# A state-space layer's tail: another home for the last decay rows, the projection's steps one output tile at a time, squares added on GpSimd, weight loads moved

## The reference, cut to what matters

```
y_f, s_f = ssd_chunked(xs, dt[:, :, 0], a[0], bm, cm, init_f)
y_b, s_b = ssd_chunked(flip(xs), flip(dt[:, :, 1]), a[1], flip(bm), flip(cm), init_b)
y = y_f + flip(y_b, 1) + xs * d_skip[:, None]
y = y.reshape(b, n, 2048) * silu(z)
y = rmsnorm(y, norm_g)
return y @ w_out, s_f, s_b          # w_out: 2048 x 1024
```

## Time and profile before

| | us |
|---|---|
| median of 3 runs | 1938.73 (1938.47 to 1939.22) |
| profiled execution | 1939.55, span 1937.7 |
| PE busy | 1842.9 (95%) |
| DVE, ACT, POOL busy | 1010.2, 605.0, 1192.1 (52%, 31%, 62%) |
| mean granted clock of TensorE | 0.982 |
| PE's longest waits in all: on the weight split (L997) | 22.3 in 7 |
| PE waits at the start of the kernel (parameters, sums) | 9.9 and 9.1 |
| PE busy in 1200 to 1410 | 181.4 of 210; from 1350 on every 10 us are 10.00 busy |
| SP's issues: rows of chunk 0 of group 3; T_O+2, T_O+3; rows of chunk 1; reload of `xT` | 1224.10; from 1233.58; 1254.69; 1327.22 |

### The profile page before, as it was taken

One profiled execution on the slowest core, in us unless ns is written; L12 is line 12 of the kernel. 1 busy time (PEld: TensorE's weight loads), 2 busy tenths in 40 slices (PEclk: granted clock), 3 DMA queues, 4 the chain that ended last, 5 costly groups with the idle time before them and its releaser, 6 DMA issues. The chain is left out here.

```text
span 1937.7 us, 33472 instructions
## 1 busy us (share of the span) xinstructions
PE 1842.9 (95%) x12857; PEld 1737.2 (90%) x12857; DVE 1010.2 (52%) x1600; ACT 605.0 (31%) x1141; POOL 1192.1 (62%) x869
## 2 busy tenths in 40 slices
PE   5999999999999999989999999976999999999997
PEld 3878899999999999989898898956999999999996
DVE  4555654563256146373666766694345623651553
ACT  4344421220022012145556657382112201220221
POOL 2533366777777777736455455514877777777773
PEclk8999999999999999999999999997999999999998
DMA  9631164424243433524333333223222222222221
GB/s 329 204 124 48 32 210 153 162 69 159 66 162 93 135 108 109 172 82 130 98 111 108 98 109 99 90 74 120 66 76 65 76 75 68 75 76 75 67 62 69
DMA packets 256189, 208.68 MB, mean 108 GB/s; under 512 B 7352, under 2 KB 235741, under 8 KB 255453
## 3 DMA queue, kind: packets, MB, share of 16 engines
q1 hardware_dynamic: 255373, 204.69, 33.5%
q10 hardware_dynamic: 720, 2.62, 0.3%
HBM read 196.63 MB, written 10.67 MB: 107 GB/s over the span
## 5 line engine op out<-in xcount | busy, mean ns | idle before, releaser
L993 POOL TENSOR_SCALAR w_hi<-raw 128x512 fp32r<-128x512 f32 (+1 forms) x432 | 643.6, 1507 | 716.8 <-PE ps L1027 530.9
L997 POOL TENSOR_TENSOR w_lo<-raw,w_hi 128x512 fp32r<-128x512 f32 (+1 forms) x432 | 555.5, 1307 | 0.0
L1027 PE MATMUL ps<-h_hi,w_hi 128*128 128x322 f32 (+1 forms) x1432 | 343.8, 321 | 4.5 <-DVE h_lo L2358 2.9
L1027 PE MATMUL ps<-h_lo,w_hi 128*128 128x322 f32 (+1 forms) x1432 | 328.5, 311 | 0.0
L1027 PE MATMUL ps<-h_hi,w_lo 128*128 128x322 f32 (+1 forms) x1432 | 328.2, 310 | 0.0
L1027 PEld LDWEIGHTS ps<-h_hi,w_hi 128*128 128x128 f32 x1432 | 241.5, 190 | 20.6 <-issue 18.3
L1027 PEld LDWEIGHTS ps<-h_hi,w_lo 128*128 128x128 f32 x1432 | 242.0, 189 | 0.0
L1027 PEld LDWEIGHTS ps<-h_lo,w_hi 128*128 128x128 f32 x1432 | 240.8, 189 | 0.0
L2249 DVE SCALAR_TENSOR_TENSOR xT<-ps,mod,xT 128x128 f32 (+1 forms) x112 | 56.6, 547 | 269.1 <-PE ps L1027 263.5
L1027 PE MATMUL ps<-g_hi,w_hi 128*128 128x322 f32 (+1 forms) x816 | 189.5, 314 | 4.5 <-POOL w_lo L997 3.1
L1027 PE MATMUL ps<-g_lo,w_hi 128*128 128x322 f32 (+1 forms) x816 | 187.6, 311 | 0.0
(11 more groups left out here) (354 smaller groups left out, 3138.4 us busy)
## 6 DMA issues: line engine op xcount, KB each, us to landing
raw<-in_ffn_w_up SPq DMA_DIRECT2D x88, 512.0 KB, 3.9
ada<-in_ada_w SPq DMA_DIRECT2D x40, 1024.0 KB, 6.5
raw<-in_ssd_w_in SPq DMA_DIRECT2D x40, 512.0 KB, 4.0
raw<-in_ffn_w_down SPq DMA_DIRECT2D x32, 512.0 KB, 3.9
R<-scr_acs SPq DMA_DIRECT2D x22, 512.0 KB, 5.3
raw<-in_att_w_in SPq DMA_DIRECT2D x16, 512.0 KB, 7.9
ada_att<-in_ada_w SPq DMA_DIRECT2D x8, 1024.0 KB, 7.2
raw<-in_ssd_w_out SPq DMA_DIRECT2D x16, 512.0 KB, 3.9
```

Source lines behind the costliest of these rows:

```text
L993: nc.gpsimd.tensor_scalar(w_hi[j % 2][:, a_:b_, :], raw[j][:, a_:b_, :], 1.0, None, ALU.mult).then_inc(w_hi_done, 1)
L997: ins = nc.gpsimd.tensor_tensor(w_lo[j % 2][:, a_:b_, :], raw[j][:, a_:b_, :], w_hi[j % 2][:, a_:b_, :].bitcast(F32), ALU.subtract)
L1027: ins = mm(out[:, cols], w[slot][:, k, :], x[:, cols], start=first and k == 0 and i == 0, stop=last and k == n - 1 and i == 2)
```

## The change

The schedule of `seg` and `yout`:

```diff
-            put(*slots[at - (0 if (g, c) == (GROUPS - 1, 1) else 2)], "seg", g, c)
+            put(*slots[at - 2], "seg", g, c)
...
-            for k, i in enumerate((9, 10, 11, 11, 13, 14, 14, 16, 17, 17, 19, 20)):
-                put(*slots[i], "yout", g, k)
+            todo = iter([(m, k) for m in range(2) for k in range(8)] + [(0, k) for k in range(8, 12)])
+            for i, n in ((9, 2), (10, 2), (11, 3), (13, 2), (14, 4), (16, 2), (17, 2), (19, 1), (20, 2)):
+                for _ in range(n):
+                    put(*slots[i], "yout", g, *next(todo))
```

A `yout` event is now one k step of one output tile (6 matmuls instead of 12): first tile 0, k 0 to 7, then tile 1, k 0 to 7, then tile 0, k 8 to 11. By slots: 9 (0,0) (0,1); 10 (0,2) (0,3); 11 (0,4) (0,5) (0,6); 13 (0,7) (1,0); 14 (1,1) to (1,4); 16 (1,5) (1,6); 17 (1,7) (0,8); 19 (0,9); 20 (0,10) (0,11). Behind the list:

```diff
-            for k in range(12, 16):
-                y_part(k)
+            for m, k in ((1, 8), (1, 9), (1, 10), (1, 11), (0, 12), (0, 13), (0, 14), (0, 15), (1, 12), (1, 13), (1, 14),
+                         (1, 15)):
+                y_part(m, k)
```

The home of `R_last` and of the odd squares, and the wait of the first load:

```diff
-        y_sums, y_sq = bT[0], (cT[0], x_tok[0][:, :, :].rearrange("p c n -> p (c n)")[:, 0:W])
+        y_sums, y_sq = bT[0], (cT[0], at("y_sq1", [P, W], F32, h_at + 12 * W * 4)[0])
...
-        R_last = at("R_last", [P, 2, GH, P], F32, aligned(h_at + 12 * W * 4))[0]
+        R_last = x_tok[0][:, :, :].rearrange("p c n -> p (c n)")[:, 0:2 * GH * P].rearrange(
+            "p (a b c) -> p a b c", a=2, b=GH)
...
                 if n == N_MID + 1:
-                    sp.wait_ge(mm_done, T_E + 40)
+                    sp.wait_ge(*ssd_end(("yd", GROUPS - 2, CHUNKS - 1)))
+                    sp.wait_ge(st_done, CS_AT[("csf", GROUPS - 2, 3)] + 1)
...
-                        after = () if n == N_MID - 2 else (n + 1, n + 2) if n in (N_MID - 1, N_MID) else (n + 2,)
-                        for i in after if n != N_MID - 1 else (n + 1,):
+                        after = () if n == N_MID - 2 else (n + 1, n + 2) if n == N_MID - 1 else (n + 2,)
+                        for i in after:
```

The rows of chunk 1 of group 3 are thus issued right behind those of chunk 0, in `beside(36)`, between the loads of T_O+1 and T_O+2. The odd squares' buffer is now the place of `y_hi` tile 12, so ACT waits before it:

```diff
                 act.wait_ge(*ssd_end(("yd", k // 4, 4)))
+                if k == 12:
+                    act.wait_ge(y_added, 11)
...
                         A_(yg[:, m, :], acc(e % 2), ACT.Silu).then_inc(acc_free_act, 1)
+                        if e == 39:
+                            A_(small[:, 15:16], ident[:, 0:1], ACT.Exp)
```

SP's order of the weight loads and the reload:

```diff
-            sp.wait_ge(*ssd_end(("yd", 3, 4)))
-            sp.wait_ge(st_stored, 128)
-            sp.dma_start(xT[:, :, :], scr_x).then_inc(x_back, 16)
-            with sp.Fori(1, 4) as i:
+            for j in range(4):
+                if j == 2:
+                    sp.wait_ge(*ssd_end(("yd", 3, 4)))
+                    sp.wait_ge(st_stored, 128)
+                    sp.dma_start(xT[:, :, :], scr_x).then_inc(x_back, 16)
+                load(j, T_O + 4 + j, w_so[:, (j % 2) * 8:(j % 2) * 8 + 8, (2 + j // 2) * P:(3 + j // 2) * P])
+            with sp.Fori(2, 4) as i:
```

POOL adds the squares of k = 1 to 11, between the splits; DVE keeps 12 to 15:

```diff
-            splits(T_E, T_END - 8)
+            def add_y_square(k):
+
+                pool.wait_ge(y_sqd, k + 1)
+                if k > 1:
+                    pool.wait_ge(y_added, k - 1)
+                nc.gpsimd.tensor_tensor(y_sums[:, :], y_sums[:, :], y_squares(k), ALU.add).then_inc(y_added, 1)
+
+            splits(T_E, T_O)
+            for j in range(2):
+                split(j, T_O + j, T_O // 4, KD)
+            for k in range(1, 8):
+                add_y_square(k)
+            split(2, T_O + 2, T_O // 4, KD)
+            for k in range(8, 10):
+                add_y_square(k)
+            split(3, T_O + 3, T_O // 4, KD)
+            for k in range(10, 12):
+                add_y_square(k)
+            splits(T_O + 4, T_END - 8)
...
-                if k:
-                    if k > 1:
-                        dve.wait_ge(y_added, k - 1)
+                if k >= 12:
+                    dve.wait_ge(y_added, k - 1)
                     tt(y_sums[:, :], y_sums[:, :], y_squares(k), ALU.add).then_inc(y_added, 1)
```

More of the change, by code:

```diff
@@ L1363, in _, with y_part @@
             ada_turn(ADA_LAST).then_inc(ada_cols, 1)
-            def y_part(k):
+            def y_part(m, k):
                 pe.wait_ge(y_ready, k + 1)
                 part = k // KD
[L1370 to L1377, removed]
+                if k % KD == 0:
+                    pe.wait_ge(w_split, T_O + 2 * part + m + 1)
+                if k == 0:
+                    pe.wait_ge(*acc_free(A_O + m - 2))
+                ins = steps(m, m, y_of(part), (k % KD,), first=part == 0, last=part == 1)
+                if k % KD == KD - 1:
+                    ins.then_inc(mm_done, 1)
             def ssd_begin(key):
@@ L1438, in _ @@
                 if kind == "yout":
-                    y_part(ev[2])
+                    y_part(ev[2], ev[3])
                 elif kind == "trB":
```

## The result

The changed kernel takes 1942.03 us (median of 19 runs, 1939.17 to 1948.39), the kernel before, run beside it, 1939.22 (19 runs). The ratio is 1.0018 with a 95% interval of 1.0011 to 1.0026: slower by 0.18%, with 2.8 us between the medians. One of the 19 runs of the kernel before took 2272.55 us, far above all others, and the ratio, which is of the fast runs, leaves it out. The time lies in the predicted range, and the likeliest case, no change, did not come: the interval lies above 1. The profiled execution took 1941.05, its span is 1939.2 (before: 1939.55 and 1937.7).

The account below looks back on a forecast made before the run. PE, 95% busy, was taken to bound the kernel, DVE setting the pace between waits in the state-space layer's end; +13.5, -12.0 and -1.8 gave -0.2 us, 1938.5 on the median, 8-in-10 range 1932.0 to 1943.5.

Parts of the forecast that it names:

- E1: Eviction of chunk 1 of group 3; forecast at 1275.8, 0.5 us later than before.
- The add's price: Squares' adds on POOL beside DVE's two-input SBUF work: 1.3 us lost each, 3.6 us taken for three in chunk 1.
- the home's 1.1 us: New home of R_last alone gives 1.1 us of the 5.4 us wait before chunk 1's product; DVE is next late.
- E1 to E2: Evictions of chunk 1 to chunk 2: PE waits for y_lo 4, stage 21.45 us, chunk 2's eviction 7.0 later than before.
- E2 to E3: Evictions of chunk 2 to chunk 3: PE waits for y_lo 7, stage 20.9 us against 14.36, +6.5.
- E3 to S: Eviction of chunk 3 to start of output tile 2: 28.4 us against 40.35, gain 12.0, weight waits mostly covered.
- S: Start of output tile 2, 1344.94 before; forecast at about 1346.
- the last term of the sum: Behind the start of output tile 2: wait of two us instead of 7.76 spares the low clock, -1.8 us.
- Z: Trace marker, no forecast: the RECIPROCAL of the last sums of squares ahead of the outputs.
- (a): Rival: adds on POOL cost DVE nothing, meeting its pauses and PSUM reads; sum -6.3, 1932.4 us; chance 0.23.
- (b): Rival: reordered steps don't hold PE up, three weight waits (19.15) and their low clock go; about 1917; chance 0.07.
- (c): Rival: slower by TensorE's clock, low for 6.1 us behind long waits, also behind short ones; +5.6, 1944.3; chance 0.15.

Follow-up runs that it names:

- b_home: The kernel before with only the new home of R_last and odd squares, its earlier load and exp, and the dummy Exp; 1938.71 us, ratio 1.0000.
- a_mix: The kernel after with projection steps in pairs to k 7 and tile by tile from k 8, adds still on POOL; 1934.95 us, ratio 0.9971.
- mix_dve: a_adds_on_dve with projection steps in pairs to k 7 and tile by tile from k 8; 1928.20 us, ratio 0.9940.
- a_adds_on_dve: The kernel after with the sums of squares back on DVE for all k, none on POOL; 1937.49 us, ratio 0.9994.
- a_fill2: The kernel after with spare matmuls in its two waits for y_lo, 28 before step (0,4) and 32 before (0,7); 1936.67 us, ratio 0.9984.
- a_early: The kernel after with 30 spare matmuls ahead of PE's first instruction, none near the tail; 1938.19 us, ratio 0.9997.
- mix_dve_early: mix_dve with 9 spare matmuls ahead of PE's first instruction; 1925.07 us, ratio 0.9928.
- a_fill: The kernel after with 9 spare matmuls in PE's wait before output tile 2; 1939.03 us, ratio 1.0003.
- b_early: The kernel before with 30 spare matmuls ahead of PE's first instruction, none near the tail; 1935.78 us, ratio 0.9979.
- b_fill: The kernel before with 30 spare matmuls in PE's wait of 7.76 us before output tile 2; 1934.54 us, ratio 0.9974.
- a_fill_all: The kernel after with spare matmuls in all its waits of the tail; 1935.58 us, ratio 0.9979.
- b_fill_all: The kernel before with spare matmuls in all its long waits of the tail; 1932.92 us, ratio 0.9965.
- a_old_steps: The kernel after with the projection's steps again in pairs, k by k, for both output tiles; 1943.03 us, ratio 1.0018.

## Why the prediction was wrong, by its own steps

**E1 right.** Predicted +0.5, measured +0.19 from chunk 0's product. The add's price was right in kind and size: 3.6 us lost to three adds forecast, 3.4 measured. By the exclusive lock of the Trainium skill ("SBUF — State Buffer", "Who interferes with whom") it would have been 4.7, an estimate: three adds of 1.55. The trace agrees that the two engines hold each other up, but the measured 1.1 each stay below that. b_home shows the home's 1.1 us: E1 1.0 earlier (19.67 against 20.69), and a wait of 5.38 still before chunk 1, released by DVE.

**E1 to E2 and E2 to E3 right.** Forecast 21.45 and 20.9, measured 21.39 and 20.56; before 14.95 and 14.36. PE started at E1+13.0 (forecast 13.8) and E2+10.7 (10.55).

**E3 to S right in kind, 1.2 us too short.** Forecast 28.4, measured 29.6, so the gain there was 10.8 us and not 12.0: POOL's split of T_O+3 ended at E3+11.4 as forecast, ACT's `y_hi` 12 came at E3+15.7 (15.0), T_O+4's split began at E3+24.1 (23.0), and PE waited 2.08 us (2). S moved +2.07, forecast +1.6. The rows of after for the two (E3 at 1315.37):

```profile
1331.05 0.83 ACT L1820 ACTIVATE y_hi<-yg,par 128x642 fp32r<-128x642 f32 x1 [13.96 <-POOL bT L1023]
```

```profile
1339.50 2.96 POOL L1000 TENSOR_SCALAR w_hi<-raw 128x512 fp32r<-128x512 f32 x2 [8.54 <-PE ps L1052]
```

**The step that failed** is the last term of the sum: "Two us of wait instead of 7.76 also spare the low clock after S: 1.8." In the profiled run the low clock under the work behind S grew instead, from 2.9 to 6.8 us, and S to the end took 1.48 us longer: 3.3 of the 3.75 us between the sum on record (-0.2) and the +3.55 counted from chunk 0's product. Before's wait of 7.76 us had taken 3.9 us of the low stretch into itself; after's of 2.08 us took none. The argument was a single row, the wait of 1.62 us that had left the pace. After a wait of 2.08 us, three traces show the low clock behind S (after, a_mix, mix_dve) and four don't (a_adds_on_dve, a_fill2, a_early, mix_dve_early). A short wait neither spares the clock nor costs it for certain. The term could come out from about -1.5 to +3 (S to Z 574.7 or 579 against before's 576.1); -1.8 lay beyond the better end of that, and I booked it as certain. With the middle, about +0.75, the sum would have been +2.3.

One trace of each kernel can't carry this alone. a_early and a_fill have after's tail up to S, b_early and b_fill before's. S lies 93.64 and 94.23 us behind chunk 0's product in the first two, 89.16 and 90.39 in the others: 4.5 and 3.8 later, not 2.07. Part of that is the clock between E2 and E3, low for 5.8 and 6.2 us behind the wait for `y_lo` 7 (2.8 in after's trace); these stages took 21.87 and 22.08 us instead of 20.56. a_early's wait and the end of its low stretch:

```profile
1305.58 0.90 PE L1052 MATMUL ps<-y_hi,w_hi 128*128 128x322 f32 x2 [7.92 <-DVE y_lo L2452]
```

```profile
1311.00:1312.00 1.00, 1.00 (x8) 1.00 (x7) 0.00 (x0) 0.00 (x0) 1.00 (x2) 0.83 0.07 16
```

There S to Z is 1.5 us shorter than b_early's, nearly what the term had said, but the gain from E3 to S is 9.1 us. So from E3 to the end, where the sum had -13.8 (-12.0 and -1.8), the pair before and after shows -9.3 and the pair b_early and a_early about -11: too much gain was booked there in either, at S or behind it.

**The rivals.** (a) is refuted by a_adds_on_dve: POOL's adds cost 0.24%. (b) is refuted by the trace: the waits for `y_lo` came, 7.06 and 7.92 us. (c), slower by the clock, named the right sign and the right places (the low level came behind both short waits, 1325.4 to 1328.8 and 1345.9 to 1352.7), but isn't the whole cause. Its long restarts stayed low for 4.8 and 2.8 us, less than its 6.1; in a_early's and a_fill's traces the second reached 5.8 and 6.2. And pairs of kernels with the same fillers, or with fillers in all long waits, keep most of the difference: a_early against b_early 0.9997 to 0.9979 (2.4 us), a_fill_all against b_fill_all 0.9979 to 0.9965 (2.7 us); the intervals overlap in both pairs, and a_fill_all's trace still has two short low stretches, from 1289.6 and 1327.1, where b_fill_all's has none. What stays there is the place of the waits: S 4.3 us later in a_fill_all than in b_fill_all, since in before's order fillers win back 3 us of S and in after's 0.7. I had given the change credit for -12.0 at S against +13.6 at E3; that they nearly cancel was right (-10.8 against +12.8), and the 0.18% is what is left of it, with a clock term whose sign I had wrong. The runs, each with its mean granted clock, tell roughly how the two share it. Within after (19 runs) as within before (108 runs, taken beside the experiments) a run takes 1.2 us less for each 0.001 of clock that it has more; the mean clocks are 0.9803 and 0.9811, the mean times 3.3 us apart. By that, an estimate from clocks listed to 0.001, the clock holds about 1 us of the difference and the waits 2.3. No experiment shows the two apart.

**The range.** It held the median, by its width: the forecast, 1938.5, was 3.5 us below. The chance for slower, 0.18, was too small, since it rested on the one row of 1.62 us against the clock.

## What to carry to other kernels

Before steps are reordered, write beside each slot which operand it needs and when that is made; a step put ahead of its operand moves a wait, and where PE waits either way only the shorter sum of waits counts (mix_dve: pairs while operands come late, tile by tile once a buffer has to be freed: -0.6%, with 9 fillers -0.8%, 1922.70 us, the fastest here). Work given to GpSimd isn't free while VectorE reads two SBUF inputs: each add of 0.74 us saved cost 1.1. A shorter wait doesn't shorten the low clock in step, for a long wait takes part of the low stretch into itself; a term that rests on the clock's level behind a wait belongs into the range, not into the sum, and an experiment that adds instructions needs a twin that adds them elsewhere.

## What the runs showed of the hardware

- A 16 KB load of instructions beside a store of 512 KB made it land in 4.4 to 5.3 us (eight kernels, before and after among them), in eleven kernels in which it fell elsewhere in 2.6 to 2.7. The Trainium skill ("Runtime: NRT & Kernel Launch", "Instruction fetch mechanics") tells of refills in 16 KiB blocks and calls their cost mostly hidden; at the end of this kernel one costs 2 to 2.5 us.
- Behind S the low clock lay under 2.9 us of work (before), 6.8 (after) or 10.2 (mix_dve), whatever the length of the wait (7.76, 2.08, 2.08 us). The longer it lasted, the longer S to Z: 573.8 to 575.0 us in the traces with none, then 576.12, 578.14 and 578.76, and 579.64 with 11.2 us (a_old_steps). What decides its length stayed open.
- Runs of one kernel differ by the clock: of after, the fastest took 1939.17 us at a mean granted clock of 0.981, the slowest 1948.39 at 0.976.
